# Rotary partners fetched by transfers within SBUF, issued from ScalarE's queue, in place of TensorE products with a signed permutation

## The reference

```
x1, x2, rest = x[..., :8], x[..., 8:16], x[..., 16:]
out = concat([x1 * cos - x2 * sin, x2 * cos + x1 * sin, rest])
```

## Time and profile before

| | |
|---|---|
| median of 3 runs | 1646.48 us (1644.31 to 1646.95) |
| the profiled execution | 1643.38 us, span 1641.5 us |
| TensorE busy | 1587.8 us, 97% of the span; mean granted clock 0.993 |
| VectorE, ScalarE, GpSimd busy | 1168.0 us (71%), 816.7 us (50%), 83.4 us (5%) |
| transfers | 293.63 MB, mean 179 GB/s |
| stretches with rotary work | 22 to 62 us, 424 to 467 us, 840 to 980 us |

### The profile page before, as it was taken

One profiled execution on the slowest core, in us unless ns is written; L12 is line 12 of the kernel. 1 busy time (PEld: TensorE's weight loads), 2 busy tenths in 40 slices (PEclk: granted clock), 3 DMA queues, 4 the chain that ended last, 5 costly groups with the idle time before them and its releaser, 6 DMA issues. The chain is left out here.

```text
span 1641.5 us, 35982 instructions
## 1 busy us (share of the span) xinstructions
PE 1587.8 (97%) x12327; PEld 1476.7 (90%) x12342; DVE 1168.0 (71%) x1780; ACT 816.7 (50%) x1343; POOL 83.4 (5%) x89
## 2 busy tenths in 40 slices
PE   8999899999999989999999999999999999999998
PEld 6987789999897868999989888889999999999997
DVE  4774779988987368888867454468767677677744
ACT  4555566653456466664445322225555355555433
POOL 2000001110300000110000000000000000000000
PEclk9999999999999999999999999999999999999999
DMA  8440435458764134446925543348555765545551
GB/s 337 159 155 1 167 116 174 170 192 272 271 224 161 42 128 161 172 167 254 351 99 179 177 156 128 116 166 309 191 180 186 245 223 176 180 168 186 184 179 51
DMA packets 81017, 293.63 MB, mean 179 GB/s; under 512 B 9008, under 2 KB 10544, under 8 KB 80176
## 3 DMA queue, kind: packets, MB, share of 16 engines
q1 hardware_dynamic: 78768, 283.31, 49.6%
q10 hardware_dynamic: 2176, 9.31, 1.6%
HBM read 291.53 MB, written 1.05 MB: 178 GB/s over the span
## 5 line engine op out<-in xcount | busy, mean ns | idle before, releaser
L946 DVE TENSOR_TENSOR WL<-ring,WH 128x1024 fp32r<-128x1024 f32 x427 | 531.5, 1246 | 271.3 <-ACT WH L467 270.0
L467 ACT ACTIVATE WH<-ring 128x1024 fp32r (+1 forms) x419 | 441.6, 1057 | 546.8 <-PE projs L1623 275.8
L1623 PE MATMUL projs<-AH,WH 128*128 128x256 f32 (+2 forms) x2120 | 541.7, 292 | 16.6 <-ACT WX L684 5.3
L1623 PE MATMUL projs<-AL,WH 128*128 128x256 f32 (+2 forms) x2120 | 531.1, 287 | 0.3
L1623 PEld LDWEIGHTS projs<-AH,WH 128*128 128x128 f32 x2120 | 400.2, 189 | 33.6 <-DVE mk L1307 13.9
L1623 PEld LDWEIGHTS projs<-AL,WH 128*128 128x128 f32 x2120 | 401.5, 190 | 5.6 <-DVE AL L1104 1.7
L1623 PE MATMUL projs<-AH,WL 128*128 128x256 f32 (+2 forms) x2192 | 315.1, 285 | 0.0
L1623 PEld LDWEIGHTS projs<-AH,WL 128*128 128x128 f32 x2192 | 285.3, 189 | 6.9 <-DVE WL L946 2.5
L1623 PE MATMUL accs<-FH,WH 128*128 (+1 forms) x768 | 190.4, 283 | 2.0 <-ACT WH L467 2.0
L1623 PE MATMUL accs<-FL,WH 128*128 (+1 forms) x768 | 189.9, 282 | 0.0
L1623 PEld LDWEIGHTS accs<-FH,WH 128*128 128x128 f32 x768 | 144.6, 188 | 3.3 <-issue 3.3
(11 more groups left out here) (261 smaller groups left out, 1890.1 us busy)
## 6 DMA issues: line engine op xcount, KB each, us to landing
ring<-in_stream SPq DMA_DIRECT2D x532, 512.0 KB, 3.3
W1v<-in_w ACTq DMA_DIRECT2D x2, 1024.0 KB, 7.3
W1k<-in_w ACTq DMA_DIRECT2D x2, 1024.0 KB, 10.1
D<-in_decay ACTq DMA_DIRECT2D x4, 512.0 KB, 4.7
x<-in_xT SPq DMA_DIRECT2D x2, 512.0 KB, 5.0
memT<-in_memT SPq DMA_DIRECT2D x1, 1024.0 KB, 11.4
ctxT<-in_ctxT ACTq DMA_DIRECT2D x1, 1024.0 KB, 7.8
out_y<-ybuf SPq DMA_DIRECT2D x8, 128.0 KB, 2.0
```

The costliest lines, as they stand in the source:

```text
L467: A(WH[:, s, :], ring[:, r % RING, :], ACT.Copy).then_inc(wh_ready, 1)
L946: V.tensor_tensor(WL[:, s, :], ring[:, r % RING, :], WH[:, s, :].bitcast(F32), ALU.subtract).then_inc(consumed, 1)
L1623: return T.matmul(out, lhsT, rhs, start=start, stop=stop, skip_group_check=True)
```

## The change

Partner rows are copied instead of multiplied. `swap` on ScalarE's queue copies the rows of P 8 partitions up or down (four transfers of 8 partitions for each part, both heads of a block), or those of Q2 and K2 64 up or down (two transfers of 64 partitions), into one new buffer, `swapped`. It first waits until the blocks are evacuated (`bank_free`) and until VectorE's sine product has read what the buffer held (`swap_used`). The sign goes into the table of sines, and sine and cosine products wait for the transfers (`in_swap`). In the first block `sine` of a part moves one step later, next to its `turned_by`. GpSimd clears `swapped` at the start. The permutation goes out of `const` and `rope2`. For K2 the first swap is issued after step 0, the products began after step 1.

```diff
-        out[:, 2 + half] = np.concatenate([np.sin(ang)] * 2)
...
+        out[:, 2 + half] = np.concatenate([-np.sin(ang), np.sin(ang)])
...
+        swapped = at("swapped", [128, 2, S], 66)
...
+                def swap(part, step, b0, nb):
+
+                    for s in range(2):
+                        act.wait_ge(bank_free[s], n["q"] + step + 2)
+                    if i or part:
+                        act.wait_ge(swap_used, 4 * i + part)
+                    else:
+                        act.wait_ge(swap_zero, 1)
+                    for r in (0, 64):
+                        for dst, src in ((r, r + 8), (r + 8, r)):
+                            act.dma_start(swapped[dst:dst + 8, 0:nb, :], P[src:src + 8, b0:b0 + nb, :]).then_inc(in_swap, 16)
+
                 def aside(step):
+                    if step == 1:
+                        swap(0, 0, 8, 1)
+                    if step == 2:
+                        swap(1, 1, 9, 2)
+                    if step == 3:
+                        swap(2, 2, 0, 2)
+                    if step == 4:
+                        swap(3, 3, 2, 2)
                     if step == 0:
...
+            def swap(rot, steps):
+
+                what, h = (Q2, K2)[rot // 4], rot % 4
+                for s in range(2):
+                    act.wait_ge(bank_free[s], n["q"] + steps + 1)
+                act.wait_ge(swap_used, 4 * DEPTH + rot)
+                for dst, src in ((0, 64), (64, 0)):
+                    act.dma_start(swapped[dst:dst + 64, :, :], what[src:src + 64, 2 * h:2 * h + 2, 0:S]).then_inc(in_swap, 16)
+
             def context(step):
+                if step < 4:
+                    swap(step, step + 1)
                 if step in (0, 1):
...
                 A(K2[:, i * 2 + s, :], proj[s][:], ACT.Copy, scale=256 ** -0.5).then_inc(bank_free[s], 1)
-            weights(K + 2, keys)
+            weights(K + 2, keys, after=lambda step: swap(4 + step, step + 1))
...
-                def sine(part, b0, nb):
-
-                    dve.wait_ge(rope_mm, 4 * i + part + 1)
-                    chain.link(V.tensor_tensor(cv[:, 0:nb, :], accs[:, part, 0:nb * S].rearrange("p (a n) -> p a n", a=nb),
-                                               rope1[:, 1, :].unsqueeze(1).to_broadcast([128, nb, S]), ALU.mult))
+                def sine(part, nb):
+
+                    dve.wait_ge(in_swap, 64 * (4 * i + part + 1))
+                    V.tensor_tensor(cv[:, 0:nb, :], swapped[:, 0:nb, :],
+                                    rope1[:, 1, :].unsqueeze(1).to_broadcast([128, nb, S]), ALU.mult).then_inc(swap_used, 1)
+                    dve.wait_ge(swap_used, 4 * i + part + 1)
...
-                    if step == 1:
+                    if step == 2:
                         if i == 0:
                             dve.wait_ge(in_rope1, 16)
-                        sine(0, 8, 1)
-                    if step == 2:
+                        sine(0, 1)
                         turned_by(0, 8, 1)
-                        sine(1, 9, 2)
                     if step == 3:
+                        sine(1, 2)
                         turned_by(1, 9, 2)
-                        sine(2, 0, 2)
                         dve.wait_ge(in_gw, 16 * (i + 1))
...
                     if step == 4:
+                        sine(2, 2)
                         turned_by(2, 0, 2)
-                        sine(3, 2, 2)
                         memory_scaled(0, 1)
...
                     if step == 5:
+                        sine(3, 2)
                         turned_by(3, 2, 2)
...
-                dve.wait_ge(rope_mm, 4 * DEPTH + rot + 1)
-                bank = (acc[2 + rot % 2] if rot < 4 else ob[rot % 2])
-                chain.link(V.tensor_tensor(cv[:], bank.rearrange("p (a n) -> p a n", a=2),
-                                           rope2[:, 128 + 2 * S:128 + 4 * S].rearrange("p (a n) -> p a n", a=2), ALU.mult))
+                dve.wait_ge(in_swap, 64 * 4 * DEPTH + 32 * (rot + 1))
+                V.tensor_tensor(cv[:], swapped[:], rope2[:, 2 * S:4 * S].rearrange("p (a n) -> p a n", a=2), ALU.mult).then_inc(swap_used, 1)
+                dve.wait_ge(swap_used, 4 * DEPTH + rot + 1)
...
+            G.memset(swapped[:], 0.0).then_inc(swap_zero, 1)
             G.memset(rows_k[:], 0.0).then_inc(zero_ready, 1)
...
-                    pool.wait_ge(rope_mm, 4 * i + part + 1)
+                    pool.wait_ge(in_swap, 64 * (4 * i + part + 1))
                     G.tensor_tensor(P[:, b0:b0 + nb, :], P[:, b0:b0 + nb, :],
...
                 for h in range(RET_HEADS):
-                    pool.wait_ge(rope_mm, 4 * DEPTH + rot + 1)
+                    pool.wait_ge(in_swap, 64 * 4 * DEPTH + 32 * (rot + 1))
                     G.tensor_tensor(what[:, 2 * h:2 * h + 2, 0:S], what[:, 2 * h:2 * h + 2, 0:S],
-                                    rope2[:, 128:128 + 2 * S].rearrange("p (a n) -> p a n", a=2), ALU.mult).then_inc(cos_done, 1)
+                                    rope2[:, 0:2 * S].rearrange("p (a n) -> p a n", a=2), ALU.mult).then_inc(cos_done, 1)
                     rot += 1
...
-                def rotated(blocks, part):
-                    for c, blk in enumerate(blocks):
-                        ins = mm(accs[:, part, c * S:c * S + S], const[:, C_ROT:C_ROT + 128], P[:, blk, :], True, True)
-                    ins.then_inc(rope_mm, 1)
-
...
-                    if step == 1:
-                        if i == 0:
-                            pe.wait_ge(in_const, 16)
-                        rotated((8,), 0)
-                    if step == 2:
-                        rotated((9, 10), 1)
+                    if step == 1 and i == 0:
+                        pe.wait_ge(in_const, 16)
                     if step in (2, 3) and i == 0:
...
                             n["norm"] += 1
-                        rotated((0, 1), 2)
                     if step == 4:
-                        rotated((2, 3), 3)
                         pe.wait_ge(gwg_ready, i + 1)
...
-            def rotated(rot):
-                what, h = (Q2, K2)[rot // 4], rot % 4
-                if rot >= 2:
-                    pe.wait_ge(rope_done, 4 * DEPTH + rot - 1)
-                bank = (acc[2 + rot % 2] if rot < 4 else ob[rot % 2])
-                for c in range(2):
-                    ins = mm(bank[:, c * S:c * S + S], rope2[:, 0:128], what[:, 2 * h + c, 0:S], True, True)
-                ins.then_inc(rope_mm, 1)
-
             def context(step):
...
                     n["norm"] += 1
-                if step == 1:
-                    pe.wait_ge(in_rope2, 16)
-                if 1 <= step <= 4:
-                    rotated(step - 1)
             make(K, X(AH), X(AL), fresh=True, after=context)
...
             pe.wait_ge(nl_ready, 8 * n["split"])
-            make(K + 2, XM(AH), XM(AL), 2 * S, after=lambda step: rotated(step + 3) if step else None)
+            make(K + 2, XM(AH), XM(AL), 2 * S)
...
                 ins.then_inc(mm_done, 1)
-                if p == 0:
-                    rotated(7)
                 if p == 2:
...
```

More of the change, by code:

```diff
@@ L109 @@
 C_ID = _take(128)
-C_ROT = _take(128)
 C_TRI = _take(128)
@@ L128, in constants @@
     c[:, C_ONES:C_ONES + 128] = 1
-    c[:, C_ROT:C_ROT + 128] = (-1.0 * ((f % 64 < 8) & (p == f + 8)) + 1.0 * ((f % 64 >= 8) & (f % 64 < 16) & (p == f - 8)))
     c[:, C_TRI:C_TRI + 128] = p <= f
@@ L152, in rope_first @@
     cos, sin = np.ones((64, S)), np.zeros((64, S))
-    cos[0:8], cos[8:16], sin[0:8], sin[8:16] = np.cos(ang), np.cos(ang), np.sin(ang), np.sin(ang)
+    cos[0:8], cos[8:16], sin[0:8], sin[8:16] = np.cos(ang), np.cos(ang), -np.sin(ang), np.sin(ang)
     t = np.stack([np.concatenate([a, a]) for a in (cos, sin)], 1)
@@ L165, in rope_second @@
         out[:, half] = np.concatenate([np.cos(ang)] * 2)
-        out[:, 2 + half] = np.concatenate([np.sin(ang)] * 2)
-    p, f = np.arange(128)[:, None], np.arange(128)[None, :]
-    rot = -1.0 * (p == f + 64) + 1.0 * (p == f - 64)
-    return np.ascontiguousarray(np.concatenate([rot, out.reshape(128, -1)], 1).astype(np.float32))
+        out[:, 2 + half] = np.concatenate([-np.sin(ang), np.sin(ang)])
+    return np.ascontiguousarray(out.reshape(128, -1).astype(np.float32))
 def decays():
@@ L303, in transformer @@
         D2 = at("D2", [128, 2, 4 * S], 72)
-        rope2 = at("rope2", [128, 128 + 4 * S], 56)
+        rope2 = at("rope2", [128, 4 * S], 56)
         ctxT = at("ctxT", [128, KB, S], 48)
@@ L340, in transformer @@
             sem(n) for n in ("gwg_ready", "gate_mm", "gates_ready", "fa_ready", "fl_ready", "fw_ready", "cc_mm", "cc_ready"))
-        rope_mm, cos_done, rope_done = sem("rope_mm"), sem("cos_done"), sem("rope_done")
+        in_swap, swap_used, cos_done, rope_done = sem("in_swap"), sem("swap_used"), sem("cos_done"), sem("rope_done")
+        swap_zero = sem("swap_zero")
         turn_mm, turned = sem("turn_mm"), sem("turned")
```

## The result

The median of nine runs is 1651.20 us (1645.83 to 1656.29), beside 1644.45 us (1643.43 to 1646.95) for the kernel before in the same session: a ratio of 1.0036, 95% interval 1.0022 to 1.0050. **The kernel became slower, by 0.36% or 6 us**, where 3.8 us faster was forecast; it lies inside the range of 1637 to 1652. Its runs scatter over 10 us, those of before over 3.5. The profiled execution took 1649.39 us with a span of 1647.5, 6.0 above the one before, so it stands for the difference, and I read it by stretches.

The account below looks back on a forecast made before the run. TensorE, busy 97% of the span, was taken as the bound, fed by ScalarE and VectorE, with VectorE nearly the bound in layer 1. Terms -2.3 + 2.9 - 0.9 - 3.5 = -3.8 us gave 1642.7 us, range 1637 to 1652.

Parts of the forecast that it names:

- the new wait: Both blocks: ScalarE's burst of transfers waits for VectorE's previous sine; bursts of four put at 2.2 us, two at 1.1.
- -2.3: Layer 0, first block: step 5 starts at 51.8, before at 54.1; -2.3 us, bounds -3.0 and +1.
- +2.9: Layer 1, first block: looped bursts delay WH and the gate product; +2.9 us, bounds -1.4 and +7.
- -0.9: Second block, Q: root, table load and split follow the last burst; -0.9 us, bounds -3.5 and 0.
- -3.5: Second block, K: the loop is 1.4 late of 4.5 allowed; -3.5 us, bounds -3.5 and -2.5.
- rival (c): First block's six loops: slow landings delay VectorE, slower from 5.7 us on; 1651.7 us at 6 us, chance 0.2.
- The ceiling: Both blocks: most that removing the products from TensorE can gain, 6.1 us in the first and 7.0 in the second.
- work taken off it is won where its feeders keep up: Three rotary stretches: TensorE, busy 97%, gains from removed work where ScalarE and VectorE keep up; ceiling 13.1 us.
- The first loop: Layer 1: sine of part 0 ends at 442.7, its burst at 445.0, and WH is ready at 446.1.
- (a): All stretches: the loops are hidden and the lower bounds hold, -11.4 us, 1635.1 us; chance 0.15.
- (b): First block: six looped sines collide with GpSimd, each costing 1.1 us more; 1649.3 us, chance 0.2.
- My own signs for error: Whole kernel: forecast fails if bursts take 3 us, sines 1.5, or VectorE's idle time ends with a DMA.

Follow-up runs that it names:

- mixed kernel: Changed kernel with three buffers in layer 0 and the second block, TensorE products kept in layer 1, `gwg` made at step 1: 1635.80 us, ratio 0.9948.
- filled kernel: Changed kernel with three buffers, plus ten products with unread results ahead of TensorE's wait for `gwg` in layer 1: 1636.87 us, ratio 0.9959.

## Why the prediction was wrong

**The step that failed is the price of the new wait**, in each term that has one. The terms -2.3, +2.9, -0.9 and -3.5 came out as -0.2, +6.3, +1.8 and -2.6: +5.3 us in place of -3.8. The waits stood where the prediction put them. Their price was too low: bursts of 2.6 to 3.2 us for 2.2, a loop of VectorE's instructions slowed by 2.1 us for 0.5, a reciprocal left out in layer 0, and the lower clock behind a stop (1.3 us in the queries) put at nothing. Three buffers, which take the wait away and nothing else, bring back 12 us and show that it was the cause. That the measured time lies inside the range is luck: the range reached so far up for slow landings, rival (c), and landings cost nothing.

**The ceiling** was 13.1 us; 6 to 7 us are to be had by taking all products away, some 8.5 by leaving those of layer 1. The price of a pair was right (0.87 us in each of the three that count in K). The step "work taken off it is won where its feeders keep up" was right as a rule and not carried through: VectorE "is nearly the bound itself" in layer 1, yet I let up to 1.4 us be won there and kept it as a bound. Without products TensorE comes 2.6 us sooner to a `gwg` that comes no sooner. With the products in their place, before and in the mixed kernel, TensorE has no such stop and the granted clock stays 1.00.

**Layer 0, -2.3 forecast, -0.2 measured.** Three terms. A burst was taken at 2.2 us from four HBM loads (0.39 at the least); it lasted 2.6 to 3.2. Sine 1 beside `rows_k` took 1.22 in place of 0.7, and with it ended at 48.2, not 47.1. And I followed the root only to ScalarE's split: VectorE's reciprocal of it stands ahead of the evacuation for which TensorE waits.

```profile
51.53 1.75 DVE L1106 RECIPROCAL rstd_m<-rms 128x256 f32<-128x256 f32 x1 [1.33 <-ACT rms L552]
53.31 0.42 DVE L1316 TENSOR_TENSOR P<-projs,rstd 128x256 f32<-128x256 f32 x1
```

```profile
53.88 0.36 PE L1652 MATMUL projs<-AH,WH 128*128 128x256 f32 x1 [2.56 <-DVE P L1316]
```

Step 5 was forecast for 51.8. In the sum for sine 1 the terms as written give 46.95 and not 47.1, and rows 7 don't show the squares that it takes from there (1.65 us, at 36.80 in the trace); neither matters beside the rest.

**Layer 1, +2.9 forecast, +6.3 measured.** The mechanism, the order and the engines of the three waits were as written (2.25, 2.62 and 0.67 us; WH, `gwg` with WH just behind, gate product). The first loop fits: WH at 446.4 for 446.1. The second is 1.6 us late at the sine (453.0 for 451.4): beside GpSimd's cosine and `rows_k` the split took 2.31, adaLN 1.74 and sine 1.20 us, where I had allowed 0.5 for all. The burst adds 0.4 in each loop. By the gate product it is 1.9 late (464.1 for 462.2). This chain runs over VectorE, so the lower clock behind the wait for `gwg` (1.5 us) lies under it here and adds nothing. The rest, 1.6 us, is one stop of TensorE in mid-piece that ends with "issue", which no forecast had:

```profile
468.89 0.28 PE L1652 MATMUL projs<-AL,WH 128*128 128x256 f32 x1 [1.62 <-issue]
```

It is 1.20 us with three buffers, 0.3 to 0.9 in six others, and absent before and in the other seven. It always stands behind the third pass of this piece, where the code has no wait. The traces' DMA records have a queue called instruction, with one packet close to this place in each run. In the eight traces with the stop it ends 1.24 to 1.42 us after this packet landed; in the others the packet landed 1.4 us or more before the pass in question. So TensorE most likely waited for its own instructions. Why they came late, and late here, stays open: no run changed it.

**Queries, -0.9 forecast, +1.8 measured,** outside the bounds of -3.5 and 0. Forecast was a wait of 2.6 behind the table load; it was 3.23, and its lower clock, passes 0.21 us apart for 2.9 us, cost 1.3 more. I priced waits at their length alone. The sine ahead of the last burst was slowed too (1.67 for 0.69 at 868.82), which is part of the longer wait. The remaining 0.8 us of the miss I haven't traced.

**Keys, -3.5 forecast, -2.6 measured.** Nothing waits for a burst, as forecast; the third pair was under cover. TensorE's idle time ahead of the V stage, put down to "issue", grew by just the 0.87 us taken out (before, then the changed kernel):

```profile
955.86 0.47 PE L1623 MATMUL accs<-WH,AH 128*128 128x512 f32 x1 [0.81 <-issue]
```

```profile
961.98 0.58 ACT L904 ACTIVATE K<-projs 128x512 f32<-128x512 f32 x1
962.66 0.47 PE L1652 MATMUL accs<-WH,AH 128*128 128x512 f32 x1 [1.68 <-issue]
```

The code has a wait there: the V stage begins only when ScalarE has evacuated the last piece of K, behind a split. The evacuation ends 0.1 us before TensorE starts, here (962.56) and before (955.77). A product ahead of that wait costs nothing, and taking it away gives nothing.

**The rivals.** (a), all loops hidden, would have been 1635.1; with three buffers, where they are hidden, it is 1638.2, by the ceiling above. (b) is a part of what happened: sines of 1.20, 1.22, 1.67 and 1.78 us, but most of its cost sits in splits and adaLN products beside `rows_k`. (c) is wrong: VectorE never idled on a landing; the cosine started 1.4 to 5.3 us after a burst's end. My own signs for error were bursts of 3 us, sines of 1.5 and DMA waits; the first two came in part, and the slip was to give each its bound alone: bursts and slowed instructions add in the ring of layer 1, and the clock in the queries.

**What stays open.** Single profiles also differ where all kernels run the same instructions: from the kernel before by 0 to +2.9 us between layer 0 and layer 1, and by -1.0 to +2.6 us between layer 1 and the queries. The granted clock differs there too. With three buffers and with the filled kernel of 1636.87 us, same window in the attention:

```profile
200.00:220.00 20.00, 18.91 (x139) 15.53 (x138) 9.61 (x17) 12.22 (x25) 0.00 (x0) 0.85 0.08 26
```

```profile
200.00:220.00 20.00, 18.49 (x145) 15.92 (x145) 10.85 (x17) 13.45 (x26) 0.00 (x0) 0.93 0.13 37
```

That a shift of the rotary stretch changes the clock granted there, and so widens the scatter of the runs, is a guess; no run tested it.

## What to carry to other kernels

Before work is taken off the busiest engine, ask in each stretch who would be late if that engine came sooner: what is behind a nearly full feeder can't be won, and is best left where it is. A transfer that has to wait for its buffer belongs in no queue that feeds the critical engine; with a second and third buffer the same transfers turned 6 us lost into 6 us won. Price a new wait with all that lies in its ring, the issues and the slowed instructions together, and keep in mind that a stop of 2 to 3 us puts the clock at risk: 1.5 us behind 13 of 22 such stops here, nothing behind the other 9.

## What the runs showed that I had not expected

- A transfer of 8 or 16 KB within SBUF takes 0.63 us to issue from ScalarE's queue and 0.52 from GpSimd's, where loads of 1 MB took 0.45 (W1k) and 0.59 to 1.34 us (W1v): the size says little about an issue.
- Idle products on a resident tile, put ahead of a wait that can't be avoided, gave 1.5 us back by TensorE's clock, twice.
- An instruction's releaser in the timeline is only the last of several: taking `gwg` out of the way uncovered WH at almost the same time.
- Two stops of TensorE that the timeline puts down to "issue" have an owner after all: a wait of the code for ScalarE's evacuation ahead of the V stage, and most likely late instructions in layer 1.
